# Queries of the second block kept without zeros; scores on a head's own 64 partitions, heads of two kinds scored in pairs

## The reference, cut to what matters

```
q, k, v = heads of (rmsnorm(x) @ w_in), 24 heads of 64       # and three gates
q, k    = first 18 heads rotated in 16 of their 64 lanes
# kind 1, heads 0..11, groups g of 4:  softmax(q k^T / 8) over t, t-d, t-2d, ...; mixed by their log-sum-exp
# kind 2, heads 12..17:                softmax(causal(q k^T / 8)) v
# kind 3, heads 18..23:  z = q k^T / 8;  a = exp(log_sigmoid(z) + suffix sum of log_sigmoid(-z)), k < q;  a v
y = gates[0] * (o_a @ w_out_a) + gates[1] * (o_b @ w_out_b) + gates[2] * (o_c @ w_out_c)
x = x + y @ w_o;  x = x + relu(rmsnorm(x) @ w_up)^2 @ w_down
```

## Time and profile before

| | |
|---|---|
| median of three runs | 1998.87 us (1997.55 to 2000.8) |
| profiled execution | 2000.66 us, span 1998.8 us |
| mean granted clock of TensorE | 0.983 of full |
| TensorE busy | 1920.0 us, 96% |
| VectorE, ScalarE, GpSimd busy | 826.4, 939.9, 1321.4 us |
| attention of block two, with its filler | 1171 to 1310 us, and 1621 to 1760 us |

### The profile page before, as it was taken

One profiled execution on the slowest core, in us unless ns is written; L12 is line 12 of the kernel. 1 busy time (PEld: TensorE's weight loads), 2 busy tenths in 40 slices (PEclk: granted clock), 3 DMA queues, 4 the chain that ended last, 5 costly groups with the idle time before them and its releaser, 6 DMA issues.

```text
span 1998.8 us, 36097 instructions
## 1 busy us (share of the span) xinstructions
PE 1920.0 (96%) x15200; PEld 1840.1 (92%) x15200; DVE 826.4 (41%) x1729; ACT 939.9 (47%) x1467; POOL 1321.4 (66%) x612
## 2 busy tenths in 40 slices
PE   6999996999999999889999999999999999999999
PEld 3999995899999998869999999989999999989999
DVE  3674676373138467735111623133311523133322
ACT  2544464344454445444444445625544445635543
POOL 0888770388878887316887865506897965506896
PEclk8999999999999999989999999999999999999999
DMA  9999660695589885317555643446664643446662
GB/s 322 362 348 313 200 190 22 207 365 176 181 276 369 303 284 180 106 50 268 191 168 181 203 152 119 134 136 188 197 203 156 198 145 122 132 135 188 200 199 98
DMA packets 357074, 398.01 MB, mean 199 GB/s; under 512 B 9016, under 2 KB 319024, under 8 KB 356912
## 3 DMA queue, kind: packets, MB, share of 16 engines
q1 hardware_dynamic: 356752, 395.50, 60.3%
q10 hardware_dynamic: 160, 0.20, 0.1%
HBM read 394.62 MB, written 1.05 MB: 198 GB/s over the span
## 4 chain that ended last, share of the span: by engine, by line
PE 89%; DVE 4%; ACT 3%; POOL 2%; SPq 1%; issue 1%; DMA 1%; ACTq 0%; DVEq 0%
PE bank L719 71%; PE bank L805 6%; PE bank L1141 3%; POOL w_lo L685 2%; PE bank L934 1%; PE bank L974 1%; SPq L547 1%; DVE bank L1669 1%; ACT arena L1356 1%; DVE arena L1740 1%; PE bank L750 1%; ACT w_hi L1220 1%; DVE arena L1784 1%; PE bank L754 1%; PE bank L710 1%
## 5 line engine op out<-in xcount | busy, mean ns | idle before, releaser
L685 POOL TENSOR_TENSOR w_lo<-ring,w_hi 128x1024 fp32r<-128x1024 f32 (+2 forms) x608 | 1321.2, 2199 | 662.5 <-ACT w_hi L1220 662.1
L719 PE MATMUL bank<-hn,w_hi 128*128 128x256 f32 x2752 | 773.6, 281 | 6.7 <-POOL w_lo L685 5.9
L1220 ACT ACTIVATE w_hi<-ring 128x1024 fp32r<-128x1024 f32 (+2 forms) x608 | 578.5, 976 | 410.6 <-PE bank L719 373.8
L719 PE MATMUL bank<-hn_lo,w_hi 128*128 128x256 f32 x2752 | 765.8, 278 | 0.0
L719 PE MATMUL bank<-hn,w_lo 128*128 128x256 f32 x2752 | 765.6, 278 | 0.0
L719 PEld LDWEIGHTS bank<-hn,w_hi 128*128 128x128 f32 x2752 | 519.0, 189 | 10.7 <-POOL w_lo L685 7.5
L719 PEld LDWEIGHTS bank<-hn,w_lo 128*128 128x128 f32 x2752 | 519.1, 189 | 0.0
L719 PEld LDWEIGHTS bank<-hn_lo,w_hi 128*128 128x128 f32 x2752 | 518.0, 188 | 1.1 <-issue 0.5
L719 PE MATMUL bank<-gated,w_hi 128*128 128x256 f32 x1408 | 248.9, 281 | 0.0
L719 PEld LDWEIGHTS bank<-gated,w_hi 128*128 128x128 f32 x1408 | 217.0, 190 | 0.0
L719 PE MATMUL bank<-gated,w_lo 128*128 128x256 f32 x704 | 197.8, 281 | 0.0
(11 more groups left out here) (212 smaller groups left out, 2133.7 us busy)
## 6 DMA issues: line engine op xcount, KB each, us to landing
ring<-in_ffn_w_in SPq DMA_DIRECT2D x88, 1024.0 KB, 7.3
ring<-in_w_in SPq DMA_DIRECT2D x72, 1024.0 KB, 5.1
arena<-in_ada_w SPq DMA_DIRECT2D x35, 2048.0 KB, 10.5
ring<-in_w_up SPq DMA_DIRECT2D x32, 1024.0 KB, 5.5
ring<-in_w_down SPq DMA_DIRECT2D x32, 1024.0 KB, 5.1
ring<-in_ffn_w_out SPq DMA_DIRECT2D x32, 768.0 KB, 5.1
ring<-in_ffn_w_out SPq DMA_DIRECT2D x32, 640.0 KB, 4.1
ring<-in_w_in SPq DMA_DIRECT2D x16, 512.0 KB, 3.7
```

Source lines behind the costliest of these rows:

```text
L685: pool.tensor_tensor(w_lo[:, q, ks], ring[:, r, k0:k0 + n], w_hi[:, q, ks], ALU.subtract) \
L719: last = mm(out, a, b, start=start and i == 0, stop=stop and i == 2)
L1220: f(w_hi[:, q, half * 4:half * 4 + n], ring[:, r, k0:k0 + n], ACT.Copy).then_inc(weights_rounded, 1)
```

## The change

Four edits, all for block two. The query tiles lose their zeros: `q2` has 12 tiles, laid out as the keys. The rotation applies the factor 1/8 within its own multiplications, and unit 5 is copied once. A soft or stick score matmul uses only the 64 partitions of its head, 0 to 63 for even and 64 to 127 for odd heads. And `scored_at` decides what a step scores: an a head as before, in its own step; of b and c heads two at every even step (b0 and b1 in step 4, c0 and c1 in step 10), with the matmuls of the two alternating, and none at the odd steps. VectorE takes the maxima of both soft heads in that step; the other operations keep their steps. Block one goes through the same function with the same operations in the same order.

```
+def scored_at(heads, i):
+    if i >= len(heads):
+        return []
+    if len(heads[i].maps) == 3 or heads[i].kind in ("diff", "fox"):
+        return heads[i:i + 1]
+    return [] if i % 2 else heads[i:i + 2]
...
-        q2 = view(0, 24, S)
+        q2 = view(0, 12, S)
...
-            def scores(hd, q, k, maps=(0, 1)):
-                for m, (qi, ki, _, _) in enumerate(hd.maps):
+            def scores(pair, q, k, maps=(0, 1)):
+                for m, (qi, ki, _, _) in enumerate(pair[0].maps):
                     if m not in maps:
                         continue
-                    sbk, free = hd.sb[m]
-                    if free:
-                        pe.wait_ge(done_by(free), eng.at(free))
...
+                    for hd in pair:
+                        sbk, free = hd.sb[m]
+                        if free:
+                            pe.wait_ge(done_by(free), eng.at(free))
+                    kind = pair[0].kind
+                    for c0, c1, keys, queries in ((0, P, slice(0, P), slice(0, P)), (P, SCW, slice(0, S), slice(P, S))):
+                        if kind == "stick":
+                            c0, c1, keys, queries = ((0, S, slice(0, P), slice(0, S)), (S, SCW, slice(P, S), slice(P, S)))[c0 // P]
+                        for hd in pair:
+                            qi, ki = hd.maps[m][:2]
+                            out = bank[:, hd.sb[m][0], c0:c1]
+                            if kind == "stick":
+                                rows = slice(64 * (qi % 2), 64 * (qi % 2) + 64)
+                                mm(out, k[rows, ki, keys], q[rows, ki, queries], start=c0 == 0, stop=False,
+                                   skip_group_check=True)
+                            elif kind == "soft":
+                                rows = slice(64 * (qi % 2), 64 * (qi % 2) + 64)
+                                last = mm(out, q[rows, ki, queries], k[rows, ki, keys], start=True, stop=True)
+                                if c0:
+                                    last.then_inc(tensor_done, eng.step(f"scores {hd.name} {m}"))
...
+                    for hd in pair if kind == "stick" else ():
+                        for c0 in (0, 256):
+                            last = mm(bank[:, hd.sb[m][0], c0:c0 + P], ident_r[:], unseen[:], start=False, stop=c0 > 0,
+                                      skip_group_check=True)
+                        last.then_inc(tensor_done, eng.step(f"scores {hd.name} {m}"))
...
             def attention(heads, q_of, tile, tt, filler):
                 for i in range(len(heads) + STEPS_AFTER):
-                    if i < len(heads):
-                        scores(heads[i], *q_of(heads[i])[:2])
+                    group = scored_at(heads, i)
+                    if group:
+                        scores(group, *q_of(group[0])[:2])
                     filler(i, 0)
...
                     if i == 5:
-                        for a in range(2):
-                            f(q2[:, 4 * i:4 * i + 4, :].rearrange("p (t a) s -> p t a s", a=2)[:, :, a], b, ACT.Identity,
-                              scale=tab("in64_eighth", 1, a)).then_inc(scalar_done, eng.step(f"z2 out {i}" if a else None))
+                        f(q2[:, 10:12, :], b, ACT.Copy, scale=0.125).then_inc(scalar_done, eng.step(f"z2 out {i}"))
...
-                    if i < len(heads):
-                        maxima(heads[i], tile, (0, 1) if three else (0, 1, 2))
+                    if i < len(heads) and heads[i].kind == "stick":
+                        maxima(heads[i], tile)
+                    else:
+                        for hd in scored_at(heads, i):
+                            maxima(hd, tile, (0, 1) if three else (0, 1, 2))
...
+                    by = 0.125 if i < 6 else 1.0
+                    dst = q2[:, 2 * i:2 * i + 2] if i < 6 else k2[:, 2 * (i - 6):2 * (i - 6) + 2]
+                    stt(by_cos[:, 0:t], src[:, 0:t], by, cosb[:, 0:t], ALU.mult, ALU.mult) \
...
+                    stt(rot[:, 0:t], rot[:, 0:t], by, sinb[:, 0:t], ALU.mult, ALU.mult) \
...
+                    tt(dst[:, 0:t], rot[:, 0:t], by_cos[:, 0:t], ALU.add) \
+                        .then_inc(vector_done, eng.step(f"rotated {i}"))
```

More of the change, by code:

```diff
@@ L908, in ffn @@
                                 f"{s} gated {PAIRS - 1}" if g == 0 else None)
[L910 to L917, removed]
@@ L919, in scores @@
-            def scores(hd, q, k, maps=(0, 1)):
-                for m, (qi, ki, _, _) in enumerate(hd.maps):
+            def scores(pair, q, k, maps=(0, 1)):
+                for m, (qi, ki, _, _) in enumerate(pair[0].maps):
                     if m not in maps:
                         continue
-                    sbk, free = hd.sb[m]
-                    if free:
-                        pe.wait_ge(done_by(free), eng.at(free))
[L926 to L938, removed]
+                    for hd in pair:
[19 more added lines that the diff above has]
+                            else:
+                                last = mm(out, q[:, qi, queries], k[:, ki, keys], start=True, stop=kind != "fox")
+                                if kind == "fox":
+                                    last = mm(out, fa[:, qi, queries], fb[:, keys], start=False, stop=True)
+                                if c0:
+                                    last.then_inc(tensor_done, eng.step(f"scores {hd.name} {m}"))
[3 more added lines that the diff above has]
+                                      skip_group_check=True)
+                        last.then_inc(tensor_done, eng.step(f"scores {hd.name} {m}"))
@@ L980, in attention @@
                 for i in range(len(heads) + STEPS_AFTER):
-                    if i < len(heads):
-                        scores(heads[i], *q_of(heads[i])[:2])
+                    group = scored_at(heads, i)
+                    if group:
+                        scores(group, *q_of(group[0])[:2])
                     filler(i, 0)
-                    if i < len(heads) and len(heads[i].maps) == 3:
-                        scores(heads[i], *q_of(heads[i])[:2], maps=(2,))
+                    if group and len(group[0].maps) == 3:
+                        scores(group, *q_of(group[0])[:2], maps=(2,))
                     filler(i, 1)
@@ L1999, in _ @@
                         .then_inc(vector_done, eng.step())
-                    tt(by_cos[:, 0:t], src[:, 0:t], cosb[:, 0:t], ALU.mult) \
+                    by = 0.125 if i < 6 else 1.0
+                    dst = q2[:, 2 * i:2 * i + 2] if i < 6 else k2[:, 2 * (i - 6):2 * (i - 6) + 2]
+                    stt(by_cos[:, 0:t], src[:, 0:t], by, cosb[:, 0:t], ALU.mult, ALU.mult) \
                         .then_inc(vector_done, eng.step(None if half else f"by cos {i}"))
+                    if half:
+                        ts(dst[:, 1], src[:, 1], by, None, ALU.mult).then_inc(vector_done, eng.step(f"by cos {i}"))
                     dve.wait_ge(vector_done, eng.at())
-                    tt(rot[:, 0:t], rot[:, 0:t], sinb[:, 0:t], ALU.mult).then_inc(vector_done, eng.step())
+                    stt(rot[:, 0:t], rot[:, 0:t], by, sinb[:, 0:t], ALU.mult, ALU.mult) \
+                        .then_inc(vector_done, eng.step())
                     dve.wait_ge(vector_done, eng.at())
[L2005 to L2020, removed]
+                    tt(dst[:, 0:t], rot[:, 0:t], by_cos[:, 0:t], ALU.add) \
+                        .then_inc(vector_done, eng.step(f"rotated {i}"))
                     dve.wait_ge(vector_done, eng.at())
```

## The result

The changed kernel took 2005.71 us, the median of 15 runs (2001.72 to 2015.32), against 2000.29 us of the kernel before (15 runs, 1993.54 to 2003.4): a ratio of 1.0036 [1.0026, 1.0047]. Run again on two other occasions it gave 1.0042 [1.0026, 1.0057] and 1.0067 [1.0046, 1.0088]. It is slower by 0.4 to 0.7%; 2000.7 us had been forecast, with a range to 2004.3.

A forecast was written before the change was run, and what follows sets the result against it. TensorE, busy 96% of the span, was taken as the bound. Per layer, pairs -3.96, switches +3.75, waits +1.46 make +1.25 us; both layers +2.5, clock -2.5, from 2000.66 to 2000.7 us; range 1996.0 to 2004.3.

The forecast's parts named there:

- Pairs side by side: Score matmuls of two heads on separate 64 partitions: 0.65 us instead of 1.31, six pairs a layer, -3.96 us.
- Rivals 2 and 3: 2: pairs run in turn, 1.31 us each, 2008.6 us, chance 0.10; 3: partly side by side, 0.86 us, 2003.2 us, 0.17.
- the 0.35 us of switches: TensorE entering and leaving 64-row matmuls once: 0.15 us in, 0.20 us out.
- Switches: TensorE going into and out of 64-row score matmuls: 9 entries and 12 exits paid, +3.75 us a layer.
- Rival 1: Switching to 64 rows costs nothing; 1995.7 us, or 1993.1 if the clock holds; chance 0.10.
- the entries of steps 12 and 14: Switches into 64-row scores at these steps, at 0.15 us each, taken as unpaid inside the new waits.
- the maxima of b1: VectorE, step 4: ahead of the scaling for a3's transposes, covered by 5.72 us of filler; cost nothing, uncovered 0.7 us.
- The waits of steps 12 and 14: TensorE waits for ScalarE's copy to free the pair's second bank: 0.73 us each, +1.46 us a layer.
- ScalarE's rounding for them is a unit ahead: Steps 12 and 14: filler and next turned tile behind the waiting matmul have their rounding done already, so no further cost.
- The clock: Step 1's wait shrinks from 2.02 to about 1.5 us, TensorE stays at 2.4 GHz: -1.27 us a layer.
- rival 4: Half clock still follows the shortened wait of step 1: 2003.2 us with both layers, 2001.9 with one; chance 0.13.
- the 1.27 us that I meant to get back: Step 1, each layer: eight score records behind the wait take 1.31 us at full clock instead of 2.58.

The follow-up runs named there:

- the order mended: Changed kernel with the maxima of a pair's second head behind the scaling of the step before on VectorE; ratio 1.0039, on another occasion 2001.84 us (1.0019).
- second profile: The changed kernel run and profiled once more, with no further edit; 2008.32 us, ratio 1.0042 against the kernel before.
- first profile: The profiled execution of the changed kernel's first series, the longest of its 15 runs: 2015.32 us.
- the reordered rounding: Order-mended changed kernel with ScalarE's rounding for the next unit ahead of the stick functions of steps 12 and 14; 2006.72 us in one run.
- the one with added maxima: Kernel before with two further maxima of b0 ahead of a3's scaling on VectorE, nothing else; ratio 1.000.
- the last experiments: Two edits of the order-mended kernel: stick heads of a pair scored one after the other, 2007.7 us; ScalarE's rounding ahead of its stick functions, 2006.72 us.

## Why the prediction was wrong, point by point

- **Pairs side by side: right.** 0.65 us and a switch for eight records (forecast 0.65, in turn 1.31). Rivals 2 and 3 were wrong. In one place pairs gained more than forecast: with the order mended, steps 4 and 5 take 15.80 us, 0.94 under before, not 0.31. The scores of step 4 stand beside a wait of TensorE for ScalarE's copies, whose end sets when the filler starts (0.41 us of wait before, 0.21 with the order mended), so the 0.35 us of switches that I charged there cost nothing.
- **Switches: right.** Steps 0 to 3 without half clock took 52.98 against 51.06 us, +1.9 for a forecast of 2.10. Rival 1 was wrong. The Trainium skill, TensorEngine Tiling, Key Properties, says that a change of the tiling mode drains TensorE; the trace agrees for the row cut too, with the 0.2 us that four score records take over their 0.65. One detail failed: I let the entries of steps 12 and 14 hide in the waits ahead of them, but the pair behind the wait takes 0.92 us, 0.27 over 0.65.
- **"In step 4 the maxima of b1 (0.7 us) now stand ahead of the scaling ... I cost it at nothing; without that cover, 0.7 us": the step that failed most.** I asked whether a delay of 0.7 us was covered and took the duration of the scaling, 1.47 us, as fixed. It was not: the scalings ended 0.3 us before GpSimd's subtraction began. The delay put two of them under it, for +4.3 us on VectorE and 1.9 to 2.1 us of wait on TensorE. The cost was shown by undoing the order: 18.08 us for steps 4 and 5 without half clock in the changed kernel (layer 0 of its second profile), 15.80 with the order mended. In the first profile half clock followed on that wait and added 1.6 us. That two were held and not one was a matter of some ns: where it was one, the forecast of no cost came out, by luck. I had named the cover and not what stood beside the moved work.
- **The waits of steps 12 and 14: right in place and size, wrong in their price.** 0.7 us each, as forecast. But "ScalarE's rounding for them is a unit ahead" was false: the rounding stands behind the stick function that waits for the late scores, and GpSimd's subtraction and the next filler behind it. That is 1.3 us a layer more, shown by the reordered rounding. The cause of the waits is narrower than I had it: both banks are asked for ahead of the first matmul. With a wait for each head they vanish, at the price of running side by side.
- **The clock: wrong, twice.** The wait of step 1 shrank as forecast, from 2.02 us to 1.51:

```profile
1198.72 0.55 PE L719 MATMUL bank<-const,arena 128*128 128x128 f32 x3 [1.51 <-ACT arena L1390]
```

  But half clock followed still (rival 4), as it did in 8 of 16 layers profiled with waits of 1.5 to 1.7 us, and in 4 of 12 with waits of 2.0 to 2.2 us: it comes and goes between executions of one kernel, and the wait's length didn't tell. And the 1.27 us that I meant to get back did not exist. TensorE's waits for ScalarE's copy in step 2 (timeline, the wait in brackets), in the kernel before and in the one with added maxima, which had no half clock in step 1:

```profile
1208.39 0.55 PE L710 MATMUL bank<-const,arena 128*128 128x128 f32 x3 [0.25 <-ACT arena L1372]
```

```profile
1208.04 0.55 PE L710 MATMUL bank<-const,arena 128*128 128x128 f32 x3 [1.72 <-ACT arena L1372]
```

What half clock takes in step 1, TensorE would wait in step 2: steps 0 to 3 take 51.14 us with it and 51.06 without. It holds for all twelve layers profiled with the a heads on 128 partitions: 51.1 to 51.5 us in the four with half clock, 51.0 to 51.5 in the eight without. In the changed kernel that wait is 0.8 to 0.9 us at most, and the same half clock costs 0.9 us (from that wait to the next, 14.0 us against 13.1), and 2.5 us in two layers of the last experiments, in which it lasted twice as long.

Added up for the first profile, a layer: 1.9 us more than forecast in steps 0 to 3, from the clock; 3.3 in steps 4 and 5; 1.9 from step 10 on. An execution with neither half clock nor a wait for held scalings has +2.4 us a layer (141.1 against 138.74). The prediction gave its own measure: wrong in the steps if the attention at full clock is not 1 to 1.5 us longer. It was 2.4 us longer with the order mended, and 4.7 in the changed kernel with the wait of step 4 (143.4). Five of six layers having the wait of 2.1 us makes some 8 us in all (an estimate from these sums), against ratios of 1.0036 to 1.0067 (5.4 to 13.7 us).

What stays open is what decides between half clock and full clock behind a wait of 1.5 to 2.2 us, and what shifts the fifth scaling by the few ns that make it held or not: no experiment here controlled either.

## What to carry to other kernels

When work is moved on one engine, look at what will run beside it on the other engines, not only at how much slack it has: here a slack of several us was used up because two instructions slid under GpSimd's. The trace of the kernel before had the same kind of operation beside such a subtraction, 1.93 us long instead of 0.35. Before a paired operation asks for two buffers at once, see whether the first one's work would have covered the second one's wait, and which orders on other engines stand behind it. And price a loss of clock by the next wait: where TensorE would wait for another engine anyway, it costs nothing, and removing it gives nothing.

## What the runs showed of the hardware

- Fp32 matmuls on partitions 0 to 63 and 64 to 127, issued alternately, run wholly side by side: with the switch, 0.86 us for the score maps of two heads and 0.85 for those of one, although a weight load is still recorded at 187 ns.
- Going to a matmul of 64 rows and back costs some 0.2 us each way. It is not hidden in a wait of TensorE ahead of it (0.92 us for a pair behind a wait, 0.85 without).
- A scaling within SBUF on VectorE that starts behind the start of a subtraction of GpSimd lasts until that instruction has ended, at most 0.2 us longer: 2.4 us instead of 0.3, and 2.13 us for a 128x2 operation. Started 4 to 7 ns behind it, the scaling kept its 0.28 us and the subtraction took 2.55 us instead of 2.40. Maxima that read PSUM were not held (0.29 and 0.42 us).
- Half clock of 3.4 us (in two layers 6.8) followed on the same wait in some executions and not in others of the same kernel.
